# One Trainium2 core, a hybrid attention and delta-rule block: the delta rule's output split into two products at two places, and two sums of squares taken in two short parts

## The chip, the cores and the metric

The kernel runs on one core of one Trainium2 chip. The metric is the device time of one launch in microseconds (us). The engines are TensorE (PE, with its weight loads PEld), VectorE (DVE), ScalarE (ACT), GpSimd (POOL) and the DMA issuer SyncE (SP). They run their own instruction lists and meet at semaphores.

## What is computed

The block takes x, 1024 tokens of width 1024, through chunked band attention (8 heads) and a gated delta rule (4 heads of 128) side by side, normalises both, multiplies by an output matrix, and ends in a SwiGLU feed-forward part. The part that matters here is the recurrence of the delta rule and the norms behind it:

```python
def step(S, inp):
    u_n, w_n, intra_n, qd_n, kd_n, gl_n = inp
    v_new = u_n - w_n @ S
    o = qd_n @ S + intra_n @ v_new
    S = S * exp(gl_n) + kd_n.T @ v_new
    return S, o
...
o = rms_norm(o, dn_out_norm_g) * silu(z)      # over the 128 of a head
a_out = rms_norm(a_out, attn_out_norm_g)      # over the 512 of the attention group
mix = concatenate([a_out, o]); x = x + mix @ w_out
```

## The kernel before

The recurrence runs over 8 tiles of 128 tokens. `dn_pe(m)`, `dn_dve(m)` and a loop on ScalarE, written out by hand, set the order; nothing is planned by a scheduler. Below, "pass m" is one call of `dn_pe(m)` (m = 1 to 7) with what VectorE and ScalarE do beside it. A pass inverts the triangular matrix of tile m (products L2164, L2171, L2178, L2185, with their masks, copies and adds on VectorE), and between these it steps the recurrence of tile m-1:

- `dn_pe_ks` (L2113): keys times state. VectorE subtracts it from the values (`dn_dve_r`).
- `dn_pe_new` (L2122): the inverse times that. ScalarE copies it out as VNEW (`dn_act_new`, L1116).
- `dn_pe_out` (L2136, L2137): for each head state times queries, then VNEW times IN added on top, into bank 5 or 7.
- `dn_pe_kv` (L2143): keys times VNEW, from which VectorE makes the next state (`dn_dve_st`, L1509).
- `dn_pe_osum` (L2152): the sum of squares of the output over a head, as one product of a matrix of ones with OSQ, both read as full float32. ScalarE squares ahead of it (`dn_act_square`, L1122) and takes logarithm and exponential behind it (`dn_act_scale`, L1127 and L1130, each with its own table load). VectorE then applies it in `dn_dve_of` (L1516) and multiplies by the gate in `dn_dve_mixed` (L1523), which writes MIX.

ORS, the tile of the scale, exists once, so the logarithm of one tile waits for `dn_dve_mixed` of the tile before. `att_sum` (L2158) is the same kind of sum for the attention group, two full float32 products of 512 columns, once, in pass 1. In passes 5 and 6 ScalarE also copies two rows of MIX to HI (L1353), and GpSimd makes LO of them (L842). Behind pass 7 stands a tail: the last tile's recurrence between blocks `out_pe(k, t)` of the output product (L414, six products of 512 columns in float32r each); the blocks of k = 4 to 7 need the last tile's MIX.

Of the kernel before, what the change touches and what calls it, by code (L numbers as in the profile page):

```python
# [15 lines left out]
F32 = mybir.dt.float32  # L16
# [142 lines left out]
def hymba_block(nc, x, gate_cols, units, gain_mix, gain_q, gain_k, bias_rev, gain_att, conv_w, a_log, dt_bias,  # L159
                gain_dn, gain_ffn, w_gate, w_up, w_down, bias_ext, bias_rows, kept, hidden, down_t, gate_table, blocks, solved, solved_t, pre, out):  # L160
    with ExitStack() as ctx:
# [57 lines left out]
        dn_layout = ([("pad_dn", [P, 7 * T + 4 * P], F32)] + [(n, [P, NHD, P], F32) for n in dn_one]  # L219
                     + [(n, [P, 2, NHD, P], F32) for n in dn_ring])  # L220
        with ExitStack() as stack:
# [10 lines left out]
        PP, VNEW, OSQ, ORS, STATE = dna[1:6]  # L232
        KD, NL, UT, IN, KN, TT = dna[6:]
# [4 lines left out]
        (proj_l, late_l, mix_l, sq_l, pre_l, inv_l, uv_l, wx_l, hb1_l, rawu_l, xr_l) = overlapped(  # L238
# [4 lines left out]
            [("pad_sq", [P, V0, T], F32), ("SQS", [P, 2, T], F32R)],  # L243
            [("pad_pre", [P, K0 + 1, T], F32), ("GR", [P, 2, NHD, P], F32), ("BR", [P, 2, NHD, P], F32),
# [14 lines left out]
        SQS = sq_l[1]  # L259
        GR, BR, DD = pre_l[1:4]  # L260
# [21 lines left out]
        ASQ, ARS = PROJ[:, V0:V0 + 2, :], PROJ[:, V0 + 2, :]  # L282
# [8 lines left out]
        gain_ffn_in = sem("gain_ffn_in")  # L291
# [126 lines left out]
        def add_rows(dve, t, bank):  # L418
# [10 lines left out]
              "sq", "sums", "ln", "rs", "mix")}  # L429
# [7 lines left out]
              "new_mm", "new", "out_mm", "kv_mm", "st", "osq", "osum", "oln", "ors", "of", "mixed")}  # L437
# [153 lines left out]
        with nc.Block() as block:  # L591
# [632 lines left out]
            def _(act):  # L1224
# [111 lines left out]
                dn_act_new(act, 0)  # L1336
                dn_act_square(act, 0)
                act.wait_ge(A["sums"], 1)
                for th in range(2):
                    act.activation(ARS[:, th * HALF:(th + 1) * HALF], ps[:, 4 + 3 * th, :], ACT.Ln, bias=eps_col[:, :],  # L1340
                                   scale=1.0 / HALF).then_inc(A["ln"], 1)
                act.wait_ge(A["ln"], 2)
                act.activation(ARS, ARS, ACT.Exp, scale=-0.5).then_inc(A["rs"], 1)
# [187 lines left out]

            def att_norm(dve, j):

                dve.wait_ge(A["rs"], 1)
                dve.scalar_tensor_tensor(out=MIX[:, j, :], in0=PROJ[:, j, :], scalar=gain_att_col[:, j:j + 1],
                                         in1=ARS, op0=ALU.mult, op1=ALU.mult).then_inc(A["mix"], 1)
# [33 lines left out]
            def dn_dve(dve, m):  # L1570

                dn_masked(dve, m, 0, 0)
                dn_masked(dve, m, 0, 1)
                dn_dve_r(dve, m - 1)
                for c in range(2):
                    dn_t_add(dve, m, c)
                if m >= 2:
                    dn_dve_of(dve, m - 2)
# [3 lines left out]
                if m >= 2:  # L1582
                    dn_dve_mixed(dve, m - 2)
                else:
                    att_acc(dve, 2)
                dn_dve_st(dve, m - 1)
                for c in range(2):
                    dn_u_add(dve, m, c)
                if 2 <= m <= 5:
                    att_norm(dve, m - 2)  # L1590
# [144 lines left out]
            def _(dve):  # L1735
# [166 lines left out]
                dn_dve_r(dve, NT - 1)  # L1902
                dn_dve_of(dve, NT - 2)
                dn_dve_mixed(dve, NT - 2)
                dn_dve_of(dve, NT - 1)
# [5 lines left out]
                for step, t in FFN_NORM_DVE:  # L1911
                    if step == "add":
                        out_add(dve, t)
                    elif step == "scale":
                        if t == 0:
                            dve.wait_ge(gain_ffn_in, 16)
# [209 lines left out]
            def dn_pe_out(pe, m):  # L2126
# [3 lines left out]
                if m == 1:  # L2130
                    pe.wait_ge(A["ln"], 2)
                ge(pe, S["of"], m - 1)
                pe.wait_ge(state_in[p], 32 * (m // 2 + 1))
                for h in range(NHD):
                    o = ps[:, dn_out_bank(m), h * P:(h + 1) * P]
                    pe.matmul(o, STATE[:, h, :], PROJ[:, DQ0 + h, tokens(m)], start=True, stop=False)  # L2136
                    mm = pe.matmul(o, VNEW[:, h, :], IN[:, p, h, :], start=False, stop=True)  # L2137
                mm.then_inc(S["out_mm"], 1)

            def dn_pe_kv(pe, m):  # L2140

                for h in range(NHD):
# [4 lines left out]
            def dn_pe_osum(pe, m):  # L2147
                pe.wait_ge(S["osq"], m + 1)
                if m == 0:
                    pe.wait_ge(A["ln"], 2)  # L2150
                ge(pe, S["oln"], m)
                pe.matmul(ps[:, osum_bank(m), :], ones_r[:, :].bitcast(F32), flat(OSQ[:, :, :]), start=True, stop=True).then_inc(S["osum"], 1)  # L2152

            def att_sum(pe):

                pe.wait_ge(A["acc"], 3)
                for th in range(2):
                    mm = pe.matmul(ps[:, 4 + 3 * th, :], ones_r[:, :].bitcast(F32), ASQ[:, 0, th * HALF:(th + 1) * HALF],  # L2158
                                   start=True, stop=True)
# [29 lines left out]
            def dn_pe(pe, m):  # L2189
# [110 lines left out]
            def _(pe):  # L2300
# [193 lines left out]
```

## Time and profile before

| | before |
|---|---|
| median of 3 runs | 1285.36 us (1283.72 to 1285.49) |
| profiled execution, span | 1281.6 us |
| what the median has around the span | 3.8 us |
| PE busy | 1265.0 us |
| DVE, ACT, POOL busy | 751.1, 581.4, 760.1 us |
| mean granted TensorE clock | 0.998 of full |
| the recurrence and its tail | 480 to 576.35 us of the span |

The profile has no launch time of its own beside the span; the 3.8 us are the median of the runs less this span. Times in rows are us from the span's start. PE 99% busy says that other engines matter only where PE waits for them, so the waits of PE are what one looks for. A full float32 product shows as two records of each instruction, a float32r product as one.

### The profile page before, as it was taken

Reading aid. Unit: us, or ns where it says so; the run is one execution under the profiler, and the core shown is the slowest. Engines: PE = TensorE matmul, PEld = TensorE weight load, DVE = VectorE, ACT = ScalarE, POOL = GpSimd, SP = SyncE. Lnnn points to the kernel's source line nnn. Section 1 sums busy time; section 2 is a strip of 40 time slices with the busy share of each in tenths; the row PEclk is TensorE's granted clock in tenths of the full one; section 3 lists DMA queues with packets and bytes.
Section 4 is the critical chain, followed back from the end, with each engine's and each line's share of the span. In section 5 each row is a group of like instructions: output and inputs, shape, how many; then the busy total and the mean of one; then the engine's idle time right before and its main releaser. Section 6 shows DMA issues by size and latency. Waiting matters only on the chain.

```text
span 1281.6 us, 18251 instructions
## 1 busy us (share of the span) xinstructions
PE 1265.0 (99%) x6908; PEld 1060.4 (83%) x6908; DVE 751.1 (59%) x1035; ACT 581.4 (45%) x932; POOL 760.1 (59%) x515
## 2 busy tenths in 40 slices
PE   8999999999999999999999999999999999999998
PEld 7888888888878888988887888888888888888887
DVE  5566656846926765743687665665644566435452
ACT  6587655652136765642453332323333324544441
POOL 4354577764426572143158996889778875654541
PEclk9999999999999999999999999999999999999999
DMA  4711354531134014542212454443344427985663
GB/s 184 259 55 35 96 154 139 147 91 50 39 82 160 3 50 144 182 169 99 83 50 89 166 221 189 161 159 127 134 175 189 189 109 268 319 289 182 202 194 147
DMA packets 83951, 185.12 MB, mean 144 GB/s; under 512 B 20937, under 2 KB 33297, under 8 KB 76825
## 3 DMA queue, kind: packets, MB, share of 16 engines
q1 hardware_dynamic: 78144, 180.22, 41.2%
q10 hardware_dynamic: 5720, 3.74, 1.0%
q8 instruction: 56, 0.92, 0.3%
q14 instruction: 31, 0.25, 0.1%
HBM read 129.58 MB, written 56.98 MB: 146 GB/s over the span
## 4 chain that ended last, share of the span: by engine, by line
PE 91%; DVE 3%; ACT 2%; POOL 2%; issue 1%; DMA 0%; ACTq 0%; DVEq 0%; POOLq 0%
PE ps L2254 29%; PE ps L391 24%; PE ps L2279 16%; PE ps L414 7%; PE ps L2071 2%; PE ps L2105 2%; PE ps L2093 1%; PE ps L2051 1%; PE ps L2034 1%; DVE SX L1832 1%; PE ps L376 1%; POOL WR L857 1%; PE ps L2136 1%; PE ps L2164 1%; PE ps L2152 1%
## 5 line engine op out<-in xcount | busy, mean ns | idle before, releaser
L391 PE MATMUL ps<-HT,SPLIT 128*128 128x512 f32 (+1 forms) x1392 | 317.5, 385 | 0.0
L391 PEld LDWEIGHTS ps<-HT,SPLIT 128*128 128x128 f32 x1392 | 252.6, 188 | 49.3
L2279 PE MATMUL ps<-S,HI 128*128 128x512 f32 x616 | 189.6, 389 | 0.0
L1036 POOL TENSOR_TENSOR S<-RAB,S 128x512 fp32r<-128x512 f32 x77 | 107.3, 1398 | 91.7 <-ACT S L1207 91.4
L2279 PEld LDWEIGHTS ps<-S,HI 128*128 128x128 f32 x616 | 115.6, 188 | 23.9
L2254 PE MATMUL ps<-S,WR 128*128 128x512 f32 x516 | 120.5, 389 | 0.0
L2279 PE MATMUL ps<-S,LO 128*128 128x512 f32 x308 | 119.8, 389 | 0.0
L1710 DVE TENSOR_TENSOR LO<-RAB,HI 128x512 fp32r<-128x512 f32 x77 | 64.4, 844 | 92.7 <-ACT HI L1204 92.6
L2254 PE MATMUL ps<-HI,WR 128*128 128x512 f32 x360 | 114.7, 389 | 0.0
L2254 PEld LDWEIGHTS ps<-S,WR 128*128 128x128 f32 x516 | 96.8, 188 | 20.3 <-POOL WR L857 0.2
L2254 PE MATMUL ps<-HI,WX 128*128 128x512 f32 x344 | 112.6, 389 | 0.6 <-ACT UV L1172 0.6
L322 POOL CAST SPLIT<-RAW 128x1024 fp32r<-128x1024 f32 x30 | 32.5, 1082 | 109.0 <-PE ps L391 108.5
L1204 ACT ACTIVATE HI<-RAB 128x512 fp32r<-128x512 f32 x77 | 48.8, 633 | 105.9 <-PE ps L2279 68.5
L987 POOL TENSOR_TENSOR SX<-SX,row_inv 128x1280 f32<-128x1280 f32 (+4 forms) x32 | 58.0, 1814 | 52.2 <-DVE row_inv L1844 51.9
L2254 PEld LDWEIGHTS ps<-HI,WR 128*128 128x128 f32 x360 | 67.6, 188 | 14.1
L2254 PEld LDWEIGHTS ps<-HI,WX 128*128 128x128 f32 x344 | 64.6, 188 | 14.4 <-issue 1.0
L857 POOL TENSOR_TENSOR WX<-RAWU,WX 128x512 fp32r<-128x512 f32 x34 | 44.1, 1309 | 52.9 <-ACT WX L1162 52.9
L324 POOL TENSOR_TENSOR SPLIT<-RAW,SPLIT 128x1024 fp32r<-128x1024 f32 x30 | 73.5, 2449 | 2.4
L2254 PE MATMUL ps<-LO,WR 128*128 128x512 f32 x180 | 70.0, 389 | 0.0
L318 POOL TENSOR_TENSOR RAW<-RAW,gain_mix_col 128x1024 f32<-128x1024 f32 x28 | 56.4, 2014 | 21.9 <-DVE PROJ L359 12.1
L2279 PEld LDWEIGHTS ps<-S,LO 128*128 128x128 f32 x308 | 57.8, 188 | 12.1
L2254 PE MATMUL ps<-LO,WX 128*128 128x512 f32 x172 | 66.9, 389 | 0.0
(285 smaller groups left out, 2563.5 us busy)
## 6 DMA issues: line engine op xcount, KB each, us to landing
hidden<-HB SPq DMA_DIRECT2D x11, 1792.0 KB, 6.6
RAB<-hidden SPq DMA_DIRECT2D x77, 256.0 KB, 3.1
RAW<-units SPq DMA_DIRECT2D x36, 512.0 KB, 3.9
RAWG<-w_gate SPq DMA_DIRECT2D x11, 1024.0 KB, 10.7
RAWU<-w_up SPq DMA_DIRECT2D x11, 1024.0 KB, 4.9
RAWD<-w_down SPq DMA_DIRECT2D x11, 1024.0 KB, 8.8
down_t<-RAWD SPq DMA_DIRECT2D x11, 1024.0 KB, 3.9
RAB<-down_t SPq DMA_DIRECT2D x44, 256.0 KB, 3.6
```

Source lines behind the costliest of these rows:

```text
L318: pool.tensor_tensor(blocks_of, blocks_of, gain_mix_col[:, :].unsqueeze(2).to_broadcast([P, KT, P]), ALU.mult).then_inc(hi_done, 1)
L322: pool.tensor_copy(dst[:, 0, :], RAW[:, slot, :]).then_inc(hi_done, 1)
L324: pool.tensor_tensor(dst[:, 1, :], RAW[:, slot, :], dst[:, 0, :].bitcast(F32), ALU.subtract).then_inc(split_done, 1)
L391: mm = pe.matmul(ps[:, bank + a // HALF, a % HALF:a % HALF + width], w, right[other][:, k, a:a + width], start=(k == order[0] and part == ...
L414: mm = pe.matmul(ps[:, bank + dh, :], left(part), unit[:, other, dh * HALF:(dh + 1) * HALF], start=(first and part == 0 and other == 0), s ...
L857: pool.tensor_tensor(weights(n)[:, 1, :], weight_whole(p, u, i), weights(n)[:, 0, :].bitcast(F32), ALU.subtract).then_inc(F["lo"], 1)
L987: pool.tensor_tensor(both, both, row_inv[:, i:i + 2].unsqueeze(2).to_broadcast([P, 2, n]), ALU.mult).then_inc(A["scaled"], 2)
L1036: pool.tensor_tensor(down_b(q, 1), RAB[:, q % RAWS, 1, :], down_b(q, 0).bitcast(F32), ALU.subtract).then_inc(R["b_lo"], 1)
L1204: act.activation(down_a(q, 0), RAB[:, q % RAWS, 0, :], ACT.Copy).then_inc(R["hi"], 1)
L1710: dve.tensor_tensor(down_a(q, 1), RAB[:, q % RAWS, 0, :], down_a(q, 0).bitcast(F32), ALU.subtract).then_inc(R["a_lo"], 1)
L2254: mm = pe.matmul(ps[:, bank, :], weights(n)[:, part, k * P:(k + 1) * P], left_block(i, other, k), start=(i in (1, 5, 6, 7 if p else 4) and ...
L2279: mm = pe.matmul(ps[:, bank + t, :], down_a(q, part)[:, t * P:(t + 1) * P], down_b(q, other), start=(p == 0 and i in (1, 6, 5, 7) and part ...
```

## The change

Four things are changed together.

1. `dn_pe_out` is taken apart. `dn_pe_from_state` (four products) stands ahead of the keys' product `dn_pe_kv`; `dn_pe_from_tile` (four products) stands behind `dn_pe_u`, the last step of the inverse.
2. `dn_pe_osum` is one tile later: pass m sums tile m-2, right behind `dn_pe_kv`. It is now two float32r products, of a rounded square and of its remainder. ScalarE squares twice, into OSQP (rounded) and into OSQ, and VectorE subtracts (`dn_dve_lo`). `att_sum` becomes four float32r products, with one more copy on ScalarE and one more subtraction on VectorE.
3. On ScalarE the scale of tile m-2 now comes between VNEW of tile m-1 and the squares of tile m-1. On VectorE `dn_dve_of` and `dn_dve_mixed` are for tile m-3, and `dn_dve_mixed` stands behind the last adds of the inverse instead of ahead of the state's update, which no longer waits for the output product.
4. In the tail the blocks with t = 2 come after all blocks with t = 0 and 1. A semaphore of a DMA is merged with another.

```diff
             def dn_act_square(act, m):
                 act.wait_ge(S["out_mm"], m + 1)
                 ge(act, S["osum"], m)
+                act.activation(OSQP[:, 0, :, :], heads(dn_out_bank(m)), ACT.Square).then_inc(S["osq"], 1)
+                ge(act, S["olo"], m)
                 act.activation(OSQ[:, :, :], heads(dn_out_bank(m)), ACT.Square).then_inc(S["osq"], 1)
...
-                for m in range(1, NT):
-                    if m > 1:
+                dn_act_new(act, 1)
+                act.wait_ge(A["root"], 2)
+                act.activation(ARS, ARS, ACT.Exp, scale=-0.5).then_inc(A["root"], 1)
+                for m in range(2, NT):
+                    if m > 2:
                         dn_act_new(act, m - 1)
-                        dn_act_square(act, m - 1)
-                    dn_act_scale(act, m - 1)
+                    dn_act_scale(act, m - 2)
+                    dn_act_square(act, m - 1)
...
+            def dn_dve_lo(dve, m):
+                dve.wait_ge(S["osq"], 2 * m + 2)
+                dve.tensor_tensor(OSQP[:, 1, :, :], OSQ[:, :, :], OSQP[:, 0, :, :].bitcast(F32), ALU.subtract).then_inc(S["olo"], 1)
...
+            def dn_pe_from_state(pe, m):
+                if m == 1:
+                    pe.wait_ge(A["root"], 2)
+                ge(pe, S["of"], m - 1)
+                for h in range(NHD):
+                    pe.matmul(ps[:, dn_out_bank(m), h * P:(h + 1) * P], STATE[:, h, :], PROJ[:, DQ0 + h, tokens(m)],
+                              start=(h == 0), stop=False, skip_group_check=True)
...
             def dn_pe_osum(pe, m):
-                pe.wait_ge(S["osq"], m + 1)
+                pe.wait_ge(S["olo"], m + 1)
...
-                pe.matmul(ps[:, osum_bank(m), :], ones_r[:, :].bitcast(F32), flat(OSQ[:, :, :]), start=True, stop=True).then_inc(S["osum"], 1)
+                for part in range(2):
+                    mm = pe.matmul(ps[:, osum_bank(m), :], ones_r[:, :], flat(OSQP[:, part, :, :]), start=(part == 0), stop=(part == 1))
+                mm.then_inc(S["osum"], 1)
...
-                dn_pe_out(pe, m - 1)
+                dn_pe_from_state(pe, m - 1)
                 dn_pe_kv(pe, m - 1)
+                if m >= 2:
+                    dn_pe_osum(pe, m - 2)
                 for c in range(2):
                     dn_pe_u(pe, m, c)
+                dn_pe_from_tile(pe, m - 1)
                 if m == 1:
                     att_sum(pe)
-                dn_pe_osum(pe, m - 1)
...
                 for k in range(4):
-                    for t in range(3):
-                        if k == 0 and t == 2:
+                    for t in range(2):
+                        if k == 0 and t == 1:
                             dn_pe_new(pe, last)
-                            pe.wait_ge(S["oln"], NT - 1)
-                            pe.wait_ge(S["of"], NT - 1)
                         out_pe(pe, k, t)
                     if k == 0:
-                        dn_pe_out(pe, last)
+                        dn_pe_from_state(pe, last)
+                        dn_pe_from_tile(pe, last)
+                        dn_pe_osum(pe, last - 1)
                     if k == 1:
                         dn_pe_osum(pe, last)
+                pe.wait_ge(S["oln"], NT - 1)
+                pe.wait_ge(S["of"], NT - 1)
+                for k in range(4):
+                    out_pe(pe, k, 2)
```

On TensorE, pass 3 from the output product to keys times state; before:

```order
551 L2136 MATMUL ps<-PROJ,STATE 128x128 [waits dn_state_in0,dn_of,dn_new]
552 L2137 MATMUL ps<-IN,VNEW 128x128
...
559 L2143 MATMUL ps<-VNEW,KD 128x128 x4
560 L2185 MATMUL ps<-UT,PP 64x64 [waits dn_half0_u,dn_half0_p]
...
564 L2152 MATMUL ps<-OSQ,ones_r 128x512 [waits dn_oln,dn_osq]
565 L2164 MATMUL ps<-TT,NL 128x64 [waits dn_half0_u,dn_ring_in0]
```

The same stretch of TensorE in the changed kernel, where L2156 is the state part, L2174 the keys' product, L2184 the sum and L2165 the chunk part:

```order
544 L2156 MATMUL ps<-PROJ,STATE 128x128 [waits dn_of]
545 L2156 MATMUL ps<-PROJ,STATE 128x128 x3
546 L2174 MATMUL ps<-VNEW,KD 128x128 [waits dn_state_in0,dn_new]
547 L2174 MATMUL ps<-VNEW,KD 128x128 x3
548 L2184 MATMUL ps<-OSQP,ones_r 128x512 [waits dn_oln,dn_olo]
549 L2184 MATMUL ps<-OSQP,ones_r 128x512
550 L2219 MATMUL ps<-UT,PP 64x64 [waits dn_half0_u,dn_half0_p]
...
554 L2165 MATMUL ps<-IN,VNEW 128x128 [waits dn_state_in0,dn_new]
555 L2165 MATMUL ps<-IN,VNEW 128x128 x3
556 L2198 MATMUL ps<-TT,NL 128x64 [waits dn_half0_u,dn_ring_in0]
```

The wait for VNEW (dn_new) has moved from the state part to the keys' product, the sum stands ahead of the inverse's last step and waits for VectorE's subtraction (dn_olo), and the chunk part stands between that step and the next pass.

On ScalarE, an ordinary pass of before (VNEW, the square, and the scale of the same tile):

```order
328 L1116 ACTIVATE VNEW<-ps 128x512 [waits dn_kv_mm,dn_new_mm]
329 L1122 ACTIVATE OSQ<-ps 128x512 [waits dn_osum,dn_out_mm]
330 L1127 ACT_TABLE_LOAD [waits dn_mixed]
331 L1127 ACTIVATE ORS<-ps,eps_col 128x512 [waits dn_osum]
332 L1130 ACT_TABLE_LOAD
333 L1130 ACTIVATE ORS<-ORS 128x512 [waits dn_oln]
```

ScalarE in the changed kernel, the pass that is the first with copies to HI (L1359), up to the next VNEW:

```order
341 L1117 ACTIVATE VNEW<-ps 128x512 [waits dn_kv_mm,dn_new_mm]
342 L1130 ACT_TABLE_LOAD [waits dn_mixed]
343 L1130 ACTIVATE ORS<-ps,eps_col 128x512 [waits dn_osum]
344 L1133 ACT_TABLE_LOAD
345 L1133 ACTIVATE ORS<-ORS 128x512 [waits dn_oln]
346 L1123 ACTIVATE OSQP<-ps 128x512 [waits dn_osum,dn_out_mm]
347 L1125 ACTIVATE OSQ<-ps 128x512 [waits dn_olo]
348 L1359 ACTIVATE HI<-MIX 128x1024 [waits dn_keys_out,att_mix]
349 L1359 ACTIVATE HI<-MIX 128x1024
350 L1117 ACTIVATE VNEW<-ps 128x512 [waits dn_kv_mm,dn_new_mm]
```

The scale has moved ahead of the squares, and in both kernels it is the table load, not the logarithm behind it, that carries the wait for the gate product (dn_mixed).

## Rows read from the trace of the kernel before

**Rows 1.** The page, busy time and share of each engine.

```profile
PE 1265.0 (99%) x6908; PEld 1060.4 (83%) x6908; DVE 751.1 (59%) x1035; ACT 581.4 (45%) x932; POOL 760.1 (59%) x515
```

**Rows 2.** Windows: length, busy PE, PEld, DVE, ACT, POOL, clock, DMA share.

```profile
480.00:576.35 96.35, 94.10 (x677) 82.12 (x676) 57.23 (x130) 52.88 (x61) 28.41 (x14) 1.00 0.51 167
576.35:1281.60 705.25, 701.43 (x3125) 580.69 (x3123) 394.19 (x419) 258.36 (x454) 463.18 (x323) 1.00 0.47 170
```

**Rows 3.** Waits, 480 to 575: engine, line, releaser: total us, times, longest.

```profile
PEld ps L2136 <- ACT VNEW L1116: 1.2, 3, 0.8
PE ps L2152 <- ACT PROJ L1340: 1.4, 1, 1.4
```

**Rows 4.** Timeline of PE, one pass: start, us, line, tiles.

```profile
509.25 1.06 PE L2143 MATMUL ps<-VNEW,KD 128*128 128x128 f32 x8
510.24 0.68 PE L2185 MATMUL ps<-UT,PP 128*64 128x64 f32 x8
510.85 1.13 PE L2152 MATMUL ps<-OSQ,ones_r 128*128 128x512 f32 x2
511.81 1.07 PE L2164 MATMUL ps<-TT,NL 128*128 128x64 f32 x8
512.72 1.11 PE L2113 MATMUL ps<-STATE,KN 128*128 128x128 f32 x8
...
515.61 0.38 PE L2178 MATMUL ps<-ident,TT 128*128 128x128 f32 x2
...
516.84 0.44 PE L2136 MATMUL ps<-PROJ,STATE 128*128 128x128 f32 x2
...
518.67 1.06 PE L2143 MATMUL ps<-VNEW,KD 128*128 128x128 f32 x8
```

**Rows 5.** Chain that ended last, output product: start, us, line, count.

```profile
562.89 17.25 PE ps L414 x76
```

**Rows 6.** Line L2158, the attention sum: ns min/median/max, first and last start.

```profile
L2158 PE MATMUL ps<-PROJ,ones_r x4: 592/592/697, 487.8 to 489.2; 128*128 128x512 f32 x4
```

**Rows 7.** Timeline of DVE, the same pass.

```profile
510.35 1.13 DVE L1509 SCALAR_TENSOR_TENSOR STATE<-STATE,EXL,ps 128x128 f32<-128x128 f32 x4 [1.84 <-PE ps L2143]
...
511.78 1.27 DVE L1535 SCALAR_TENSOR_TENSOR MIX<-PROJ,gain_att_col 128x1024 f32<-128x1024 f32 x1
...
514.91 0.74 DVE L1516 SCALAR_TENSOR_TENSOR ORS<-ps,gdn_col,ORS 128x512 f32<-128x512 f32 x1
...
517.24 0.68 DVE L1523 TENSOR_TENSOR MIX<-ORS,PROJ 128x512 f32<-128x512 f32 x1
```

**Rows 8.** Timeline of ACT, one pass, and the copies to HI.

```profile
518.88 0.60 ACT L1122 ACTIVATE OSQ<-ps 128x512 f32<-128x512 f32 x1 [2.47 <-PE ps L2137]
519.49 1.28 ACT L1127 ACT_TABLE_LOAD   x1
521.43 0.69 ACT L1127 ACTIVATE ORS<-ps,eps_col 128x512 f32<-128x512 f32 x1 [0.66 <-PE ps L2152]
522.14 1.28 ACT L1130 ACT_TABLE_LOAD   x1
523.43 0.63 ACT L1130 ACTIVATE ORS<-ORS 128x512 f32<-128x512 f32 x1
...
533.40 1.99 ACT L1353 ACTIVATE HI<-MIX 128x1024 fp32r<-128x1024 f32 x2
```

**Rows 9.** Line L1297, its table load, and what its engine sat idle for.

```profile
L1297 ACT ACT_TABLE_LOAD  x1: 1283/1283/1283, 349.5 to 349.5; - x1
...
  DVE YB L1499: 16.5, 1
```

**Rows 10.** Timeline, pass 6: gate product on DVE beside GpSimd's LO.

```profile
534.52 5.13 POOL L842 TENSOR_TENSOR LO<-MIX,HI 128x1024 fp32r<-128x1024 f32 x2 [23.80 <-ACT HI L1353]
...
536.10 1.34 DVE L1523 TENSOR_TENSOR MIX<-ORS,PROJ 128x512 f32<-128x512 f32 x1
```

**Rows 11.** Tile UT, its loads, 480 to 560.

```profile
DMA to landing us min/median/max: 2.6/2.8/3.2
```

More of the change, by code:

```diff
@@ L217, in hymba_block @@
         dn_ring = ["KD", "NL", "UT", "IN", "KN", "TT"]
-        dn_layout = ([("pad_dn", [P, 7 * T + 4 * P], F32)] + [(n, [P, NHD, P], F32) for n in dn_one]
+        dn_layout = ([("pad_dn", [P, 6 * T + 4 * P], F32), ("OSQP", [P, 2, NHD, P], F32R)] + [(n, [P, NHD, P], F32) for n in dn_one]
                      + [(n, [P, 2, NHD, P], F32) for n in dn_ring])
@@ L231, in hymba_block @@
         PT, SX = att
-        PP, VNEW, OSQ, ORS, STATE = dna[1:6]
-        KD, NL, UT, IN, KN, TT = dna[6:]
+        OSQP, PP, VNEW, OSQ, ORS, STATE = dna[1:7]
+        KD, NL, UT, IN, KN, TT = dna[7:]
         WO = outs[0]
@@ L428, in hymba_block @@
              ("room", "acc", "gt_turned", "masked", "scores", "biased", "prob", "turned", "pt0", "pt1", "pv", "inv", "scaled", "ao",
-              "sq", "sums", "ln", "rs", "mix")}
+              "sq", "split", "sums", "root", "mix")}
         G = {n: sem("gate_" + n) for n in ("in", "act", "dve", "cum", "back", "zero")}
@@ L436, in hymba_block @@
               "pre_out", "keys_out", "block_out", "solve", "ks_mm", "r",
-              "new_mm", "new", "out_mm", "kv_mm", "st", "osq", "osum", "oln", "ors", "of", "mixed")}
+              "new_mm", "new", "out_mm", "kv_mm", "st", "osq", "olo", "osum", "oln", "ors", "of", "mixed")}
         rows_in = [sem("dn_rows_in0"), sem("dn_rows_in1")]
@@ L1336, in _ @@
                 dn_act_new(act, 0)
+                act.wait_ge(A["acc"], 3)
+                act.activation(ASQP[:, 0, :], ASQ[:, 0, :], ACT.Copy).then_inc(A["split"], 1)
                 dn_act_square(act, 0)
@@ L1576, in dn_dve @@
                     dn_t_add(dve, m, c)
-                if m >= 2:
-                    dn_dve_of(dve, m - 2)
+                if m == 1:
+                    att_acc(dve, 2)
+                if m >= 3:
+                    dn_dve_of(dve, m - 3)
                 for c in range(2):
@@ L1902, in _ @@
                 dn_dve_r(dve, NT - 1)
+                dn_dve_lo(dve, NT - 2)
+                dn_dve_of(dve, NT - 3)
+                dn_dve_mixed(dve, NT - 3)
                 dn_dve_of(dve, NT - 2)
                 dn_dve_mixed(dve, NT - 2)
+                dn_dve_lo(dve, NT - 1)
                 dn_dve_of(dve, NT - 1)
@@ L2124, in dn_pe_new, with dn_pe_from_tile @@
                 mm.then_inc(S["new_mm"], 1)
-            def dn_pe_out(pe, m):
+            def dn_pe_from_state(pe, m):
+                if m == 1:
+                    pe.wait_ge(A["root"], 2)
[3 more added lines that the diff above has]
+                              start=(h == 0), stop=False, skip_group_check=True)
+            def dn_pe_from_tile(pe, m):
                 p = m % 2
                 pe.wait_ge(S["new"], m + 1)
-                if m == 1:
-                    pe.wait_ge(A["ln"], 2)
-                ge(pe, S["of"], m - 1)
                 pe.wait_ge(state_in[p], 32 * (m // 2 + 1))
                 for h in range(NHD):
-                    o = ps[:, dn_out_bank(m), h * P:(h + 1) * P]
-                    pe.matmul(o, STATE[:, h, :], PROJ[:, DQ0 + h, tokens(m)], start=True, stop=False)
-                    mm = pe.matmul(o, VNEW[:, h, :], IN[:, p, h, :], start=False, stop=True)
+                    mm = pe.matmul(ps[:, dn_out_bank(m), h * P:(h + 1) * P], VNEW[:, h, :], IN[:, p, h, :],
+                                   start=False, stop=True, skip_group_check=True)
                 mm.then_inc(S["out_mm"], 1)
             def dn_pe_kv(pe, m):
+                pe.wait_ge(S["new"], m + 1)
+                pe.wait_ge(state_in[m % 2], 32 * (m // 2 + 1))
                 for h in range(NHD):
@@ L2147, in dn_pe_osum @@
             def dn_pe_osum(pe, m):
-                pe.wait_ge(S["osq"], m + 1)
+                pe.wait_ge(S["olo"], m + 1)
                 if m == 0:
-                    pe.wait_ge(A["ln"], 2)
+                    pe.wait_ge(A["root"], 2)
                 ge(pe, S["oln"], m)
-                pe.matmul(ps[:, osum_bank(m), :], ones_r[:, :].bitcast(F32), flat(OSQ[:, :, :]), start=True, stop=True).then_inc(S["osum"], 1)
+                for part in range(2):
+                    mm = pe.matmul(ps[:, osum_bank(m), :], ones_r[:, :], flat(OSQP[:, part, :, :]), start=(part == 0), stop=(part == 1))
+                mm.then_inc(S["osum"], 1)
             def att_sum(pe):
-                pe.wait_ge(A["acc"], 3)
+                pe.wait_ge(A["split"], 2)
                 for th in range(2):
-                    mm = pe.matmul(ps[:, 4 + 3 * th, :], ones_r[:, :].bitcast(F32), ASQ[:, 0, th * HALF:(th + 1) * HALF],
-                                   start=True, stop=True)
+                    for part in range(2):
+                        mm = pe.matmul(ps[:, 4 + 3 * th, :], ones_r[:, :], ASQP[:, part, th * HALF:(th + 1) * HALF],
+                                       start=(part == 0), stop=(part == 1))
                 mm.then_inc(A["sums"], 1)
```

30 lines of the change are left out of this document (17 added, 13 removed).

## The prediction

> **What bounds the kernel now.** I read the page first: TensorE is busy for 1265.0 of 1281.6 us [rows 1]. So work taken from TensorE counts in full, and everything else counts only by what TensorE then waits for. The windows say where to look: the recurrence with its tail has 94.10 busy us in 96.35, everything behind it 701.43 in 705.25, and the clock is 1.00 in both [rows 2]. The second stretch is untouched by the change and follows TensorE, so I take it to move as a whole. The list of waits names what TensorE waits for in the first: 1.4 us for the attention group's logarithm ahead of the first head sum, and 1.2 us in three waits for VNEW [rows 3]. The timeline of a pass shows no gap: from one keys' product to the next it takes 518.67 - 509.25 = 9.42 us [rows 4].
>
> **TensorE's work.** The float32 head sum takes 511.81 - 510.85 = 0.96 us [rows 4]. A float32r product of 512 columns takes 17.25 / 76 = 0.227 us in a row of them [rows 5], so two take 0.46. Were they not to overlap, the pair would cost up to the old 0.96; I take 0.46, since the row is of the same shape. Gain 0.50 each, 8 times: 4.0. The attention sum has four records over 487.8 to 489.2, so 0.47 each and 1.9 together [rows 6]; four short products take 0.91. Gain 0.95. The halves of the output product (516.84 to 518.67, 1.83) only change place, 0.92 each. Together **-4.95**, and a pass becomes 8.92.
>
> **Old waits.** In pass 1 nothing needs the attention logarithm until the state part of pass 2: from the attention sum's end 516.84 - 511.81 = 5.0 us of inverse, keys times state and new values go by first [rows 4], against 0.2 + 2 x 0.69 + one table load, some 3 us, on ScalarE [rows 8]. The waits for VNEW go too, since the state part (0.92) now stands over the copy (0.60). **-2.6** [rows 3].
>
> **The new loop.** The logarithm of tile m-2 waits for the gate product of tile m-3, which VectorE now does at the end of pass m, behind the state's update. In order from the start of a keys' product: 1.10 to the update (509.25 to 510.35), 1.43 for update and adds (to 511.78), the gate product 0.68 and a hop of 0.05 [rows 4, 7]. Then ScalarE: load to next start 1.29, logarithm 0.71, load 1.29, exponential 0.63, two squares 1.20, VNEW 0.60 [rows 8], and the next keys' product, which waits for VNEW. The sum is 8.98, some 8.95 with the small overlaps of neighbours. That is level with TensorE's 8.92. The other branch (exponential, 0.74 for `dn_dve_of`, the state part 0.92) is 8.84 before hops, level too. So ordinary passes have no slack and nearly no wait; I put nothing on them.
>
> Whether the first load stands in this loop decides 1.29 us per pass. In the rows the load ran early, at 519.49, right behind the square, while the logarithm waited until 521.43 [rows 8]. But the instruction order has the wait for the gate product on the load itself, and line L1297 shows such a load: its engine sat idle 16.5 us until VectorE's YB, and the load began then [rows 9]. Before, the gate product was long done; now it is late. I take the load as held.
>
> The pace of loads is also where a page speaks against this change. The row shows 523.43 - 522.14 = 1.29 from a load to its activation, and 0.01 between the square's end and the load [rows 8]. The Trainium skill (ScalarE: Activation LUTs, What ACT_TABLE_LOAD costs) gives 1.283 us for the load and a drain of 1.38 on top, 2.66 in all. The first figure agrees with the trace, the drain does not show. By the page as an estimate the loop would be 2.76 longer in each of five passes and the time near 1301; I go by the rows.
>
> **Where the loop waits.** Passes 5 and 6 put the two copies to HI (1.99, 1.9 with overlap [rows 8]) into the full loop, behind the squares and ahead of VNEW. Before, they cost 0.2 each (1.2 less the longest 0.8, in two [rows 3]). Keys' product of pass 6: **+1.9**. GpSimd's LO starts one copy later and lasts 5.13 [rows 10], so from 1.5 ahead of that keys' product to 3.6 behind it; the gate product stands 2.5 behind it and takes 1.34 beside LO, not 0.68 [rows 10]. So pass 7: 1.9 + 0.65, **+2.55**. Unslowed, it is 1.9.
>
> Tail, first wait: from the last but one keys' product, the state part of tile 7 needs `dn_dve_of` of tile 5, for which VectorE first does the remainder of tile 6. 2.53 + 1.38 (gate product beside LO, hop) + 1.29 + 0.71 + 1.29 + 0.63 + 1.20 + the remainder 0.60 (nearest row the gate product's 0.68, less overlap) + 0.74 = 10.4. TensorE gets there in 0.95 + 0.46 + 0.61 + 0.92 + 0.95 + 0.95 + two blocks of 6 x 0.227 = 7.5 [rows 4, 5]. **+2.9**.
>
> Second: the last sum stands two blocks behind the sum before it. From the state part TensorE reaches it in 0.92 + 0.92 + 0.46 + 2.72 = 5.0. Its operand needs the other sum (2.3, 0.2 until released), 0.71 + 1.29 + 0.63, `dn_dve_of` 0.74, gate product 0.69 and remainder 0.69: 7.2. **+2.2**, hidden by nothing.
>
> **Hidden.** The second square and the remainder are in the sums above. The blocks of k = 4 come 12 x 1.36 = 16 us behind the last sum and need scale, gate, one copy and one LO, some 9 us. UT of a tile is issued at the end of a new-values product and needed about 5.1 us on (5.6 before); it lands in 2.6 to 3.2 [rows 11]. IN, KD and behind them on SP's queue TT and NL are issued 2 us later in a pass, because the chunk part is; they are needed a whole pass on. In pass 1 the attention additions stand on VectorE ahead of the state's update, about 0.2 to 0.5 us late against a slack of 0.8 in front of pass 2, which the chunk part and the sum fill.
>
> **Sum.** -4.95 - 2.6 + 1.9 + 2.55 + 2.9 + 2.2 = +2.0 on a span of 1281.6. With the same 3.8 us around it: 1283.6 + 3.8 = **1287.4**. A measurement of this kernel can tell 0.2% (2.6 us) from no change. So work goes away and waits of the same size come: no change that can be told.
>
> **Rivals.**
> - *Forecast*, 52 in 100: 1285.5 to 1289.5, from 0.2 us less or more on each of the four waits, the +0.65 absent, and 0.1 us of hops per pass.
> - *The load is not held*, 13 in 100: 1.29 less in the loop. Ordinary passes gain slack, the four waits become 0.6, 1.25, 1.6 and 2.2, and the sum is -1.9: 1283.5. [rows 8] have an early load for it, [rows 9] speak against it.
> - *The waits are covered*, 8 in 100: the copies to HI fit into slack that I don't see, and only the tail's last wait is left: -4.95 - 2.6 + 2.2, 1280.0.
> - *Slower*, 22 in 100: the loop, not TensorE, sets every pass. It has nine links, and 8.95 against 8.92 holds only if each hop is as short as in these rows. With 0.5 us more per pass (one gate product slowed by GpSimd's splitting, or hops of 0.1), five passes add 2.5: 1290. It decides from 0.12 us per pass on; the place is the keys' product waiting for VNEW in passes 3 and 4, or the state part waiting for `dn_dve_of`.
> - *A switch of tables costs more behind its own wait* than the 0.01 us in the rows, 2 in 100: at 0.6 us (one activation more) per load, 1.2 per pass and tail, seven times, gives 1296. Its place is the loop of every pass. In kind it is the drain of the Trainium skill (ScalarE: Activation LUTs, What ACT_TABLE_LOAD costs).
> - Rest, 3 in 100: a load lands late, or TensorE's clock falls in a gap of 3 us (it did not in the old 1.4).
>
> **Chances.** Faster: 8 and a third of the 13, 12. Slower: 22, 2 and a quarter of the forecast (13), whose range reaches above 1288, 37. The rest, 51, within 0.2%. Range: the forecast's whole range, the unheld load's centre and the slower loop's, 1283.2 to 1290.6, about 8 in 10.
>
> **What would show it.** In the changed profile: sums of two records 0.23 apart; no wait for the attention logarithm; the keys' products about 8.95 apart, then 10.8 and 11.5; the load ahead of the logarithm starting at the gate product's end, 2.5 + 0.7 behind the keys' product; in the tail gaps of about 2.9 ahead of the state part and 2.2 ahead of the last sum. It is wrong if the loads start right behind VNEW, if keys' products stay 8.9 apart in passes 6 and 7, or if ordinary passes are over 9.1.

## The result and the profile after

| | changed kernel | kernel before, same chip |
|---|---|---|
| median | 1289.75 us (5 runs, 1287.06 to 1291.37) | 1284.05 us (5 runs, 1283.72 to 1285.49) |
| ratio, 95% interval | 1.0040 (1.0029 to 1.0051) | 1 |
| profiled execution, span | 1288.0 us, clock 0.999 | 1281.6 us |

The change makes the kernel 0.4% slower, 2.4 us beyond the predicted 1287.4 and inside its range. The page has less work on TensorE, and more span:

```profile
span 1288.0 us, 18269 instructions
PE 1262.6 (98%) x6908; PEld 1059.3 (82%) x6908; DVE 756.4 (59%) x1044; ACT 585.0 (45%) x941; POOL 759.4 (59%) x515
```

The windows (columns as in [rows 2]; cut where the first block of k = 4 starts, 580.81 now and 576.35 before) say where the idle time is:

```profile
480.00:580.81 100.81, 91.65 (x668) 82.41 (x668) 66.42 (x138) 56.81 (x70) 31.34 (x15) 0.98 0.49 157
580.81:1288.00 707.19, 702.27 (x3125) 580.52 (x3123) 388.05 (x417) 258.22 (x454) 458.58 (x322) 1.00 0.48 169
```

TensorE now idles 9.2 us in the first stretch, where it idled 2.3 [rows 2]. From the first TensorE product of pass 1 to the blocks of k = 4 it took 97.0 us before and takes 102.4 now: +5.4. The other 1.0 of the spans' 6.4 lies in stretches that the change doesn't touch (0.9 less ahead of it, 1.9 more behind it); the stretch behind takes 704.0 to 707.2 us in the twelve profiled executions of this document, and the changed kernel's is the longest of them.

What is waited for, 480 to 576, in the list of waits (us in total, times, longest):

```profile
ACT L1130 <- DVE MIX L1534: 24.3, 7, 6.1
...
PE ps L2156 <- DVE ORS L1527: 3.3, 2, 2.7
...
PE ps L2174 <- ACT VNEW L1117: 2.8, 2, 1.4
...
PE ps L2184 <- DVE OSQP L1522: 2.1, 1, 2.1
```

Both groups of [rows 3] are gone. In their place, the logarithm's table load (L1130) waits seven times for the gate product, and TensorE waits at the state part (L2156), the keys' product (L2174) and the last head sum (L2184). The timeline of TensorE has the places; the keys' products mark the passes:

```profile
493.82 1.06 PE L2174 MATMUL ps<-VNEW,KD 128*128 128x128 f32 x8
...
502.78 1.06 PE L2174 MATMUL ps<-VNEW,KD 128*128 128x128 f32 x8
503.59 0.71 PE L2184 MATMUL ps<-OSQP,ones_r 128*128 128x512 f32 x2
504.23 0.68 PE L2219 MATMUL ps<-UT,PP 128*64 128x64 f32 x8
...
506.40 1.10 PE L2198 MATMUL ps<-TT,NL 128*128 128x64 f32 x8 [0.40 <-DMA UT<-solved]
...
508.91 1.10 PE L2205 MATMUL ps<-PP,UT 128*128 128x64 f32 x8 [0.46 <-DVE PP L1564]
...
513.30 1.06 PE L2174 MATMUL ps<-VNEW,KD 128*128 128x128 f32 x8
...
522.34 1.06 PE L2174 MATMUL ps<-VNEW,KD 128*128 128x128 f32 x8
...
532.95 1.16 PE L2174 MATMUL ps<-VNEW,KD 128*128 128x128 f32 x8 [1.40 <-ACT VNEW L1117]
...
541.91 1.16 PE L2156 MATMUL ps<-PROJ,STATE 128*128 128x128 f32 x8 [0.67 <-DVE ORS L1527]
544.47 1.16 PE L2174 MATMUL ps<-VNEW,KD 128*128 128x128 f32 x8 [1.40 <-ACT VNEW L1117]
...
554.99 1.51 PE L2156 MATMUL ps<-PROJ,STATE 128*128 128x128 f32 x8 [2.67 <-DVE ORS L1527]
556.30 1.91 PE L2165 MATMUL ps<-IN,VNEW 128*128 128x128 f32 x8
557.87 1.20 PE L2184 MATMUL ps<-OSQP,ones_r 128*128 128x512 f32 x2
558.87 1.17 PE L415 MATMUL ps<-SPLIT,HI 128*128 128x512 f32 x4
...
563.90 0.73 PE L2184 MATMUL ps<-OSQP,ones_r 128*128 128x512 f32 x2 [2.06 <-DVE OSQP L1522]
```

Passes 3 to 7 take 8.96, 10.52, 9.04, 10.61 and 11.52 us. (UT in the rows of pass 4 is a tile of the inverse that comes in by DMA, PP a masked product that VectorE writes.) In ScalarE's timeline each load stands held behind the gate product:

```profile
512.32 0.60 ACT L1117 ACTIVATE VNEW<-ps 128x512 f32<-128x512 f32 x1
516.58 1.28 ACT L1130 ACT_TABLE_LOAD   x1 [3.66 <-DVE MIX L1534]
517.88 0.69 ACT L1130 ACTIVATE ORS<-ps,eps_col 128x512 f32<-128x512 f32 x1
518.58 1.28 ACT L1133 ACT_TABLE_LOAD   x1
```

From the load to its logarithm it is 1.30 us, as in [rows 8], and from the logarithm's end at 518.57 to the next load 0.01. The drain of 1.38 us that the Trainium skill (ScalarE: Activation LUTs, What ACT_TABLE_LOAD costs) adds to a load does not show behind a held load either.

The state part of pass 5 and `dn_dve_of` ahead of it show what sets pass 5:

```profile
520.54 0.75 DVE L1527 SCALAR_TENSOR_TENSOR ORS<-ps,gdn_col,ORS 128x512 f32<-128x512 f32 x1 [1.06 <-ACT ORS L1133]
521.35 1.16 PE L2156 MATMUL ps<-PROJ,STATE 128*128 128x128 f32 x8
```

VectorE and GpSimd, pass 4 and the first pass with copies to HI (one view each). L323 and L325 are GpSimd's split of one unit of the output matrix (512 KB) into a rounded part and a remainder:

```profile
504.91 0.47 DVE L1584 TENSOR_TENSOR UT<-ps,UT 64x128 f32<-64x128 f32 x2
505.31 2.15 DVE L1534 TENSOR_TENSOR MIX<-ORS,PROJ 128x512 f32<-128x512 f32 x1
...
508.58 0.48 DVE L1564 TENSOR_TENSOR PP<-ps,level_mask 128x128 f32<-128x128 f32 x2
...
535.59 1.48 DVE L1534 TENSOR_TENSOR MIX<-ORS,PROJ 128x512 f32<-128x512 f32 x1
```

```profile
503.45 1.04 POOL L323 CAST WO<-RAW 128x1024 fp32r<-128x1024 f32 x1 [18.22 <-DMA RAW<-units]
504.56 2.35 POOL L325 TENSOR_TENSOR WO<-RAW,WO 128x1024 fp32r<-128x1024 f32 x1
531.54 4.97 POOL L843 TENSOR_TENSOR LO<-MIX,HI 128x1024 fp32r<-128x1024 f32 x2 [24.63 <-ACT HI L1359]
```

### The profile page after: what moved, and what is told of

It reads as the page before. It is cut to its first block, busy times and chain, and to the rows that moved or that the text cites. A ratio compares the mean times of both kernels' runs of the same rounds, so it can differ in the third digit from the quotient of the medians.

```text
span 1288.0 us, 18269 instructions
## 1 busy us (share of the span) xinstructions
PE 1262.6 (98%) x6908; PEld 1059.3 (82%) x6908; DVE 756.4 (59%) x1044; ACT 585.0 (45%) x941; POOL 759.4 (59%) x515
## 4 chain that ended last, share of the span: by engine, by line
PE 86%; DVE 6%; ACT 3%; issue 2%; POOL 2%; DMA 1%; ACTq 0%; DVEq 0%
PE ps L2290 28%; PE ps L392 23%; PE ps L2315 15%; PE ps L415 6%; PE ps L2095 2%; PE ps L2129 1%; PE ps L2117 1%; PE ps L2058 1%; PE ps L2075 1%; DVE SX L1852 1%; PE ps L377 1%; POOL WR L858 1%; PE ps L2198 1%; DVE LO L1730 1%; PE ps L2083 1%
## 5 line engine op out<-in xcount | busy, mean ns | idle before, releaser
L323 POOL CAST SPLIT<-RAW 128x1024 fp32r<-128x1024 f32 x30 | 32.6, 1087 | 108.9 <-PE ps L392 108.4
L325 POOL TENSOR_TENSOR SPLIT<-RAW,SPLIT 128x1024 fp32r<-128x1024 f32 x30 | 73.4, 2448 | 2.4
```

What stands on the lines that cost most here:

```text
L323: pool.tensor_copy(dst[:, 0, :], RAW[:, slot, :]).then_inc(hi_done, 1)
L325: pool.tensor_tensor(dst[:, 1, :], RAW[:, slot, :], dst[:, 0, :].bitcast(F32), ALU.subtract).then_inc(split_done, 1)
```

## The experiments

All ratios are to the kernel before. e1 to e4, e9 and e10 edit the changed kernel; e5 joins e2 and e4, and e6 to e8 edit e5.

**e1, the load loosened.** A one-column logarithm ahead of the waits pulls the table load behind VNEW.

```diff
             def dn_act_scale(act, m):
+                act.activation(row_sum[:, 0:1], eps_col[:, :], ACT.Ln)
                 act.wait_ge(S["osum"], m + 1)
```

> Changed kernel with a logarithm of one column ahead of each scale's waits, so that the table load runs right behind VNEW and no longer waits for the gate product. Loop theory (VectorE's gate product, held load, ScalarE, VNEW set the passes): 1.3 us less in each loop, so the waits for VNEW ahead of the keys' products of passes 6 and 7 fall from 1.4 and 1.4 to about 0.1 and 0.8 (with the wait ahead of the state part of pass 7 gone), the tail's first wait from 2.7 to 1.4, the last stays 2.1: 4 to 5 us faster than the changed kernel, equal to before or up to 0.1% faster. Rival 1 (VectorE's extra subtraction and late transfers fill the passes): within 1 us of the changed kernel, 0.3 to 0.4% slower than before. Rival 2 (only the fallen clock in the tail costs): the clock still falls behind any wait of over 1 us, little changes.

1284.22 us, ratio 1.0001 (0.9991 to 1.0010). ScalarE's timeline:

```profile
512.00 0.60 ACT L1117 ACTIVATE VNEW<-ps 128x512 f32<-128x512 f32 x1
512.62 1.28 ACT L1128 ACT_TABLE_LOAD   x1
513.91 0.20 ACT L1128 ACTIVATE row_sum<-eps_col 128x1 f32<-128x1 f32 x1
517.23 0.69 ACT L1131 ACTIVATE ORS<-ps,eps_col 128x512 f32<-128x512 f32 x1 [3.12 <-DVE MIX L1535]
```

The load stands 0.02 behind VNEW and the logarithm alone waits. TensorE's waits for VNEW fall from 1.40 each to 0.21 and 0.51, the state part's from 0.67 and 2.67 to 0.86 once; two of 0.4 appear at the head sum, where VectorE's remainder for it now meets GpSimd's LO and takes 2.41 and 2.71 us instead of 0.68. Pass 4 still takes 10.32, and the last wait, 2.09, is untouched.

**e2, the loop cut.** Two scale tiles in turn (ORSS, the second one in space that was padding), so that the logarithm waits for the gate product one tile further back.

```diff
-                ge(act, S["mixed"], m)
+                ge(act, S["mixed"], m - 1)
+                ORS = ORSS[m % 2]
```

> Changed kernel with two tiles for the scale in turn, so that the logarithm of a tile waits only for the gate product two tiles before. Loop theory: the gate product leaves the loop altogether; no waits for VNEW in passes 6 and 7 and none ahead of the tail's state part, pass 4 shorter by 1 us or more, the last wait of 2.1 stays: 6 to 8 us faster than the changed kernel, ratio to before 0.997 to 0.999. Rival 1 (VectorE's work and late transfers): unchanged, 1.004. Rival 2 (clock alone): without the wait of 2.7 no fall of the clock, 2 us better at most, 1.002.

1279.80 us, ratio 0.9969 (0.9959 to 0.9979). TensorE's timeline:

```profile
512.26 1.06 PE L2178 MATMUL ps<-VNEW,KD 128*128 128x128 f32 x8
521.22 1.06 PE L2178 MATMUL ps<-VNEW,KD 128*128 128x128 f32 x8
530.18 1.06 PE L2178 MATMUL ps<-VNEW,KD 128*128 128x128 f32 x8
539.14 1.06 PE L2178 MATMUL ps<-VNEW,KD 128*128 128x128 f32 x8
554.01 0.73 PE L2188 MATMUL ps<-OSQP,ones_r 128*128 128x512 f32 x2 [2.12 <-DVE OSQP L1524]
```

With the loop gone, passes 5 to 7 take 8.96, copies to HI or not, and the tail's first wait is gone. Pass 4 keeps 10.03 and the last wait 2.12: neither is mainly the loop's.

**e3, the copies to HI moved behind VNEW.**

```diff
                         dn_act_new(act, m - 1)
+                    if m in (6, 7):
+                        act.wait_ge(A["mix"], 2 * m - 10)
+                        act.wait_ge(S["keys_out"], 32 * NT)
+                        for k in (2 * m - 12, 2 * m - 11):
+                            act.activation(HI[:, k, :], MIX[:, k, :], ACT.Copy).then_inc(mix_hi, 1)
                     dn_act_scale(act, m - 2)
                     dn_act_square(act, m - 1)
-                    if m in (5, 6):
...
```

> Changed kernel with the two pairs of copies to HI moved from behind the squares to right behind VNEW of the next pass, where ScalarE sat idle for 3.7 us ahead of the load. Loop theory: the waits of 1.4 us for VNEW in passes 6 and 7 go (some 3 us), the tail's first wait (2.7) and last (2.1) stay, since GpSimd still runs beside the gate product: ratio to before 1.001 to 1.003. Rival 1 (the passes are full on ScalarE as a whole): the copies cost the same wherever they stand, 1.004.

1284.19 us, ratio 1.0008 (1.0000 to 1.0017). Passes 6 and 7 take 9.04 and 9.41 instead of 10.61 and 11.52, with no wait for VNEW. Their load begins 2.1 us after the copies' end and still waits for the gate product, so the copies fill time that was idle. Both tail waits stay (2.21, 2.09). Pass 4, which this edit doesn't touch, takes 9.60 here against 10.52 in the changed kernel, with no wait for UT or PP; its gate product takes 1.13 against 2.15. So the length of pass 4 differs from one execution to the next by up to 0.9 us.

**e4, the tail's order.** Two more blocks ahead of the state part, two more ahead of the last sum.

```diff
+                out_pe(pe, 0, 0)
+                dn_pe_new(pe, last)
+                out_pe(pe, 0, 1)
+                out_pe(pe, 1, 0)
+                out_pe(pe, 1, 1)
+                dn_pe_from_state(pe, last)
+                dn_pe_from_tile(pe, last)
+                dn_pe_osum(pe, last - 1)
+                for k in (2, 3):
+                    for t in range(2):
+                        out_pe(pe, k, t)
+                dn_pe_osum(pe, last)
```

> Changed kernel with the tail's eight early blocks spread otherwise: two more blocks ahead of the last tile's state part, four between the two last sums. Loop theory: the waits of 2.7 and 2.1 us are filled with work that was to be done anyway, and the clock stays at its upper level: 4.7 us less, and 1.6 more where the clock fell: ratio to before 0.999 to 1.001. Rival 2 (clock fell for another reason): 4.7 us less only in waits, clock still at half for some us.

1282.14 us, ratio 0.9986 (0.9977 to 0.9995). Both tail waits are gone, and the chunk's products in the tail take their usual time:

```profile
556.58 1.16 PE L2156 MATMUL ps<-PROJ,STATE 128*128 128x128 f32 x8
...
558.92 1.09 PE L415 MATMUL ps<-WO,HI 128*128 128x512 f32 x4
```

556.58 to 558.92 is 2.34 us; the changed kernel took 558.87 - 554.99 = 3.88 for the same products. The changed kernel's windows show why (the clock is third from the end):

```profile
556.00:557.00 1.00, 1.00 (x7) 1.00 (x6) 0.00 (x0) 1.00 (x1) 0.00 (x0) 0.50 0.08 16
...
558.00:559.00 1.00, 1.00 (x5) 0.81 (x4) 0.00 (x0) 0.00 (x0) 0.00 (x0) 0.50 0.00 0
```

**e5, e2 and e4 together.**

> The two scale tiles and the respread tail together. Loop theory: with the gate product out of the loop (worth 0.7% against the changed kernel) and the tail's last wait of 2.1 us filled, and no fall of the clock: 2 to 4 us less than with two scale tiles alone, ratio to before 0.994 to 0.9955. Rival (the gains overlap, both only remove the tail's waits): 0.9965 to 0.998.

1278.38 us, ratio 0.9952 (0.9939 to 0.9964). From 480 to 572 TensorE idles 0.25 us in 92 and the clock is 1.00; the first 70 of these:

```profile
480.00:550.00 70.00, 69.75 (x584) 65.19 (x584) 52.54 (x131) 45.89 (x57) 20.27 (x9) 1.00 0.53 172
```

**e6, e5 with one load late.** The load of the output matrix's fifth unit moves on SyncE's queue from pass 3 to pass 6.

```diff
-                    if m == 3:
+                    if m == 6:
```

> As e5_best, with the fifth unit of the output matrix loaded three passes later, so that neither its transfer nor GpSimd's splitting of it falls into pass 4. If these two make pass 4 long (10.0 us between keys' products instead of 9.0 with two scale tiles: UT landed late, attention products and masks on VectorE late), pass 4 falls to 9.0 and up to 0.5 us comes back in pass 7 from a late UT: 0.5 to 1 us less than e5_best, ratio 0.0004 to 0.0008 lower. If pass 4 is long for another reason, the time is that of e5_best.

1277.11 us, ratio 0.9949 (0.9936 to 0.9963), not told from e5. Pass 4 falls from 9.54 to 8.96, and pass 7 rises from 8.97 to 9.51 with a wait of 0.28 for UT: the cost moved with the load.

**e7, e5 with long sums.** The head sums are again one full float32 product of OSQ; the second square and the remainder on the other engines are kept.

```diff
-                for part in range(2):
-                    mm = pe.matmul(ps[:, osum_bank(m), :], ones_r[:, :], flat(OSQP[:, part, :, :]), start=(part == 0), stop=(part == 1))
-                mm.then_inc(S["osum"], 1)
+                pe.matmul(ps[:, osum_bank(m), :], ones_r[:, :].bitcast(F32), flat(OSQ[:, :, :]), start=True, stop=True).then_inc(S["osum"], 1)
```

> As e5_best, but the eight head sums are again one full float32 product each, of the unrounded square; ScalarE still squares twice and VectorE still subtracts, with nothing reading the results; the attention sum stays in short parts. The sum of the prediction: 0.50 us more in each of eight sums with TensorE the bound again, 4.0 us, ratio 0.0031 above e5_best. Rival (the float32r pair saves little since products of another type follow each other): under 1.5 us, 0.001.

1280.67 us, ratio 0.9967 (0.9956 to 0.9977). Keys' products come 9.36 apart instead of 8.96: a short pair saves 0.40 us in a pass. Over the whole recurrence it is less than eight times that: 92.99 us against e5's 91.15, since pass 4 takes 9.54 in both and the tail's two sums save 0.31 together. The intervals of e5 and e7 overlap; the trace tells them apart.

**e8, e5 with the output product joined.** In the passes the chunk part stands right behind the state part again.

```diff
                 dn_pe_from_state(pe, m - 1)
+                dn_pe_from_tile(pe, m - 1)
                 dn_pe_kv(pe, m - 1)
...
-                dn_pe_from_tile(pe, m - 1)
```

> As e5_best, but in the passes the chunk part of the output stands right behind the state part again, ahead of the keys' product, so that the output product is in one piece. TensorE has the same work. The keys' product is 0.9 us later against the pass and only 0.5 + 0.6 us of work stand between it and the next pass, against 1.4 us of state update and adds: 0.3 to 0.5 us of wait ahead of each pass, 2 to 4 us in all, ratio 0.0015 to 0.003 above e5_best. Rival (the place of the chunk part does not matter, only the short sums and removed waits do): the time of e5_best.

1279.73 us, ratio 0.9963 (0.9949 to 0.9976), not told from e5. In the trace the inverse's next product waits five times for VectorE's additions:

```profile
507.30 1.07 PE L2202 MATMUL ps<-TT,NL 128*128 128x64 f32 x8 [0.42 <-DVE UT L1588]
```

Passes take 9.43 to 9.62 where e5 has 8.96. The chunk part's new place is thus worth about 0.5 us per pass: it covers those additions. Over the whole recurrence e8 takes 92.74 us and e5 91.15.

**e9, the changed kernel with e6's edit alone.**

> The changed kernel, with only the load of the output matrix's fifth unit moved on SyncE's queue from pass 3 to pass 6, so that GpSimd's split of it no longer lies beside pass 4's gate product. Theory A (the gate product of a loop without slack, slowed to 2.15 us by GpSimd, holds the table load and so VNEW): pass 4's keys' products come 9.0 us apart instead of 10.52 and its gate product takes 0.7 us; 1.5 us saved in the loop, or about 1288.2. Whatever the split meets where it now lies (passes 6 and 7 already run beside GpSimd's LO) may take some of it back. Rival B (UT landing late, 3.7 us, made pass 4 long): pass 4 stays near 10.5. The tail's two waits and the clock's fall stay in both.

1287.94 us, ratio 1.0035 (1.0021 to 1.0048), not told from the changed kernel. Pass 4 takes 9.04 and its gate product 0.67. But this moved two things: the split on GpSimd, and the transfer in front of UT.

**e10, the split alone held back.** The load stays where it is.

```diff
+                    if k == 4:
+                        pool.wait_ge(S["mixed"], 3)
                     if k == 6:
                         pool.wait_ge(S["mixed"], NT)
```

> The changed kernel, with the load of the output matrix's fifth unit left where it is and only GpSimd's split of it held back, until the gate product of pass 5. It parts the two causes that the late load took away together in pass 4 (10.52 us, against 8.96). Theory A (the gate product beside the split, 2.15 us, makes VectorE's masks late): its share goes, TensorE's wait for PP of 0.46 with it, and pass 4 takes about 9.6 to 9.8 us; what stays is the wait for UT (0.4 to 0.6), whose load is issued 2.9 us behind the unit's transfer and lands 5.6 us later. Rival B (UT alone): pass 4 stays near 10.5. Rival C (the gate product alone): pass 4 takes about 9.0. In time 0.7 to 0.9 us under the changed kernel, less than rounds can tell: the verdict is the trace's.

1287.17 us, ratio 1.0032 (1.0019 to 1.0044), not told from the changed kernel either. The keys' products, and pass 4's gate product in VectorE's timeline:

```profile
502.40 1.06 PE L2176 MATMUL ps<-VNEW,KD 128*128 128x128 f32 x8
511.44 1.06 PE L2176 MATMUL ps<-VNEW,KD 128*128 128x128 f32 x8
```

```profile
504.93 0.67 DVE L1536 TENSOR_TENSOR MIX<-ORS,PROJ 128x512 f32<-128x512 f32 x1
```

Pass 4 takes 9.04, all of its excess gone. One execution would not do for that, since the passes of the changed kernel show 10.52, 10.45 (e4) and 9.60 (e3) for pass 4. But in the three executions with the split elsewhere it is 9.04 (e9, e10) and 8.96 (e6), and in the six with the same products in a pass and the split in its place (the changed kernel, e1 to e5) 9.54 to 10.52, so the split is what makes pass 4 long, and rival C holds. The wait for UT is less clear. With the unit's transfer 2.89 us ahead of it, UT landed in 4.7 to 5.7 us in the seven executions with the split in place, and in 4.9 in e10, which lies among them; e3 (5.2) and e7 (4.7) have the split and no wait for UT. That the split makes UT land later is not shown.

The same execution has something else to say. Its tail waits are those of the changed kernel, and the clock did not fall (third from the end of the windows' row):

```profile
553.14 1.16 PE L2158 MATMUL ps<-PROJ,STATE 128*128 128x128 f32 x8 [2.67 <-DVE ORS L1529]
```

```profile
552.00:556.00 4.00, 2.86 (x21) 2.67 (x22) 1.78 (x3) 1.76 (x3) 0.00 (x0) 1.00 0.02 4
```

## Why the prediction was right, and where it was short

The waits came where they were forecast, but the likeliest case, +2.0 us in the recurrence and no change that can be told, was too small: the recurrence takes +5.4 and the kernel is 0.4% slower, clear of the noise, which had 37 in 100. 1289.75 lies just above the forecast's own 1285.5 to 1289.5 and beside the 1290 of the slower rival, and that is luck: the rival had 0.5 us in each of five passes, and what came was 1.56 in one pass and 1.5 from the clock. One of the prediction's own signs of being wrong appeared, an ordinary pass over 9.1 (pass 4).

| step | predicted | measured |
|---|---|---|
| TensorE's work | -4.95 | -4.1 |
| old waits | -2.6 | -2.6 |
| pass 4, pass 5 | 0, 0 | +1.56, +0.08 |
| pass 6, pass 7 | +1.9, +2.55 | +1.65, +2.56 |
| tail, two waits | +2.9, +2.2 | +2.67, +2.06 |
| clock in the tail | 0 | +1.5 |
| sum | +2.0 | +5.4 |

Passes are counted over 8.96; the clock's 1.5 is 3.88 less 2.34. TensorE's -4.1 is what is left of the measured 5.4 when the other rows are taken away. Its parts agree: six passes at 0.46 less (9.42 to 8.96), 0.31 in the tail (e7) and about 1.0 in the attention sum (four records in 1.98 us before, 1.01 from start to start now) make 4.1. The rows for pass 4 and the clock are of one execution.

- **The held load was right.** The load starts 3.28 us behind the keys' product (516.58 - 513.30, predicted 3.26), and e1 shows its price: with the load freed, all that the change had lost comes back (ratio 1.0001). I had 3.9 between the forecast and the unheld load. By the medians it is about 5, by the two profiles 3.75 in the recurrence (98.64 us against 102.39), so the size of 3.9 is borne out as far as this can be told.
- **The loop with no slack was right, by the other branch.** Once the loop is full, an undisturbed pass takes 9.04 (pass 5; passes 4 and 5 of e9), set not by VNEW but by `dn_dve_of` and the state part behind it: 520.54 + 0.75 = 521.29, and the state part starts at 521.35. The prediction had this branch at 8.84 before hops, so it was 0.2 short. TensorE alone needs 8.96 (e2), predicted 8.92.
- **The copies to HI were right.** e2 and e3, by different means, each take the waits of passes 6 and 7 away.
- **Both tail waits were right in place and within 0.25 in size**; e4 removes both.
- **"A float32r product takes 0.227 us, so two take 0.46" was mis-sized.** That row is from a chain of 76 products in a row. Where the pair stands alone between short products it takes 0.64 from start to start (503.59 to 504.23), and the saving is 0.40 in a pass (e7), not 0.50. The whole pass still fell by 0.46, the other 0.06 by the new order of the products, so most of the missing 0.85 is in the tail's two sums.
- **"I put nothing on ordinary passes" failed in pass 4.** I knew the gate product beside LO (1.34) and moved that slowing into pass 7, but did not look at what else GpSimd has running under the new place of the gate product. The split of the fifth unit stood there: 2.15 us instead of 0.67, the masks behind it late, a wait for PP of 0.46, and beside these one for UT of 0.40. The two waits are 0.86 of the 1.56; the rest is in the products right behind them and in the state part, which starts 0.27 late. The slower rival named this cause at 0.5 us and put its place at the table load's loop; it was mostly VectorE's order that passed it on (e2 has no such loop and still takes 10.03). In e3, with a gate product of 1.13 and no such waits, pass 4 is 9.60 all the same.
- **"UT lands in 2.6 to 3.2" failed for the same pass.** I moved SyncE's ring loads 2 us and held them for harmless, without the 512 KB unit that is issued among them. The unit is now issued 2.89 us ahead of UT (497.91 and 500.80) where it was 4.57 (501.80 and 506.37), and UT takes 5.6 us to land. At 4.7 to 5.2 us (e7, e10, e3) it was not waited for.
- **The clock** had a part of 3 in 100 "in a gap of 3 us". It fell after one of 2.67. "It did not in the old 1.4" is true of the gap in pass 1; but behind another gap of 1.36 us, ahead of the recurrence, it did fall in the kernel before's own profile (below).

The rival that the load is not held would have given 1283.5; e1, which makes it true, gives 1284.2. The drain doesn't show in the rows above.

Against the median, 1289.75 is 5.7 over the kernel before on the same chip; 5.4 is what the recurrence shows. The rest lies within the 3.2 us by which the untouched stretch behind differs between executions.

## What to carry to other kernels

When a step moves, look at what the other engines run under its new place, not only at its own queue: one split beside one VectorE operation cost 1.5 us in the profiled execution, and 0.6 to 1.5 in others. Read a wait where the instruction stream has it: a table load may hold the wait of the activation behind it, and one column of dummy work or a second buffer then pays more than the change did. Work taken from the bound engine is worth its size only if the loop through the other engines is shorter; the same change with two scale tiles and another tail order is 0.5% faster than before (e5) instead of 0.4% slower.

## What the runs showed of the hardware

- **TensorE's clock fell behind some idle gaps and not behind others of the same length.** In the changed kernel TensorE idled 2.67 us, started at 554.99, and from 556 to 559 the granted clock was 0.50, 1.2 GHz of 2.4; behind its second gap, 2.06, it stayed at 1.00. e10 had the same gaps, 2.67 and 2.07, and stayed at 1.00 behind both; e9 (2.65 and 2.12) fell behind both. Of the ten gaps of 2.06 to 2.67 us in six profiled executions, six were followed by such a fall. Shorter gaps can be too: ahead of the recurrence every one of the twelve executions has a gap of 1.36 us, at about 385 us, and in four of them (the kernel before, e4, e5 and e7) the clock fell behind it, in the kernel before to 0.50 from 387 to 389. So such a gap costs its length and, in some executions, more besides: 1.5 us in the tail of the profiled one. What decides it is open. Over the five executions of the changed kernel the mean clock is 0.997 to 1.000 and the time goes with it, 1287.06 us at 1.000, 1290.40 and 1291.37 at 0.997, but a mean doesn't say in which stretch the clock fell.
- **The gate product waits for GpSimd's operation to end, and does not run slower beside it.** It has both operands in SBUF and takes 0.67 us alone. In pass 4 it ends at 505.31 + 2.15 = 507.46, which is 0.55 behind the end of the split (504.56 + 2.35 = 506.91); in the first pass with LO it ends at 537.07, 0.56 behind LO's end (531.54 + 4.97 = 536.51). In the seven executions in which the split is under way when the gate product of pass 4 begins, that product takes 1.13 to 2.27 us and ends 0.54 to 0.55 behind the split each time. So its price is what is left of GpSimd's operation, and 2.15, 1.48 and 0.67 are one mechanism at three moments. It goes the other way too. In the kernel before, VectorE was first by 0.05 us, and it was the split that took longer, 2.85 instead of 2.35:

```profile
507.82 0.68 DVE L1523 TENSOR_TENSOR MIX<-ORS,PROJ 128x512 f32<-128x512 f32 x1
507.87 2.85 POOL L324 TENSOR_TENSOR WO<-RAW,WO 128x1024 fp32r<-128x1024 f32 x1
```

Which is first can't be read from the start times alone: in e9 a gate product that starts 0.30 behind an LO takes its 0.68, and the LO takes 3.20 instead of 2.35. An operation that reads ps (UT<-ps,UT at 504.91) took its usual 0.47 us beside the same split. The Trainium skill (SBUF — State Buffer, SBUF: two separate sides) calls the port that VectorE and GpSimd share an exclusive lock for the whole instruction, taken by VectorE's operations with two SBUF inputs; the trace agrees in these places, and no run tells this port from another cause of such a wait.
